# An encoder block on one core: the opening rebuilt in four column quarters, and the two first weight tiles of a norm three steps apart

## The chip, the core and the metric

The kernel runs on one core of a Trainium2 chip. Its engines are TensorE (PE: matmuls; PEld in the profile is its weight load), VectorE (DVE), ScalarE (ACT), GpSimd (POOL) and SyncE (SP, here only an issuer of transfers). Each works through its own list of instructions in order, and semaphores tie the lists together. SBUF is the working memory with 128 partitions, PSUM holds eight banks (pb0 to pb7) into which TensorE writes. The metric is the device time of one execution in microseconds (us), the median of several.

## What is computed

A residual block over 512 tokens of width 1024: a half-step SwiGLU FFN, a mixer (short convolution and latent attention), a second half-step FFN, a final norm. Each part is preceded by an RMS norm whose result is scaled and shifted by vectors that come from a conditioning vector c. What the change touches is the first three lines below.

```python
mod = (jax.nn.silu(c) @ ada_w[l] + ada_b[l]).reshape(b, N_MOD, D_MODEL)   # 1024 x 9216 weights
sh1, sc1, g1 = mod[:, 0], mod[:, 1], mod[:, 2]
h = modulate(rmsnorm(x, norm_ffn1_g[l]), sh1, sc1)          # h*(1+sc1)+sh1
x = x + 0.5 * g1[:, None, :] * swiglu(h, ffn1_w1[l], ffn1_w3[l], ffn1_w2[l])
h = modulate(rmsnorm(x, norm_mix_g[l]), sh2, sc2)
z = h @ w_in[l]
...
h = modulate(rmsnorm(x, norm_ffn2_g[l]), sh3, sc3)
x = x + 0.5 * g3[:, None, :] * swiglu(h, ffn2_w1[l], ffn2_w3[l], ffn2_w2[l])
return rmsnorm(x, final_norm_g)
```

## The kernel before

The order on every engine is written out by hand. x is kept transposed (features on partitions) as xres, eight tiles of 128x512. Every fp32 product is made from three matmuls of a faster number format (`three`, L711): a value is split into a high part and the rest, for weights (raw to wh on ACT in `split_hi`, then wl = raw - wh on DVE or GpSimd) and for activations (hh on ACT, hl on DVE). A weight tile ("unit") takes 8 steps of three matmuls with 512 columns. Two buffers of each kind alternate, so a unit's split waits until the unit two before it is done (unit_done).

The opening, up to the loop of FFN1:

- SP (L264 on) issues constants, positions, x in one transfer of 2 MB, ten small vectors and a constant, then ada_start in eight transfers of 1 MB (scale's 1024x1024 weights, then shift's), then the first two weight tiles raw0 and raw1.
- TensorE turns the vectors (L803) and x (L811, 32 transposes), copies going to xres on ACT (L465). It multiplies a part of the modulation weights itself: `ada_columns` (L813 to L822) takes k-tiles 0 and 1 of scale, and 0 to 2 of shift, with a 128x128 block of weights as the stationary operand and one column of silu(c) as the moving one.
- DVE accumulates the other k-tiles in acc (128x1024, `ada`, L1183 and L1185), then transposes in 32x32 blocks and reduces (`fold`, L1192, L1195), and TensorE adds up the rest (`mod_columns`, L834). `mod_bias` makes mods of it.
- ACT squares each tile of xres (L412), GpSimd adds the eight squares up (L357), TensorE sums over partitions (`norm_sum`, L736), ACT takes the root (L417), DVE the inverse, and `norm_spread` (L754) spreads it over the partitions into pb7.
- `apply` (L1158 and L1151): u = x * a * spread, hh = u + shift on ACT (L429), hl on DVE. The shift vector is made between tile 2 and tile 3 of u.
- Then `first_pair` (L763): the two first units, whose steps alternate, b = 0 and b = 1 for each k, as each tile of hh and hl comes. It is used three times: FFN1, the mixer's projection, FFN2.
- `warm` (L758) issues matmuls of 384 columns whose result is not used.

The loops of FFN1, FFN2 and their second halves then run with TensorE as the engine that sets the pace; the other seven modulation vectors are made in FFN1's loop from ada_ring, whose transfers GpSimd issues once mods_ready is 2.

## Time and profile before

| | us |
|---|---|
| median of 3 runs | 1050.64 |
| lowest, highest | 1049.11, 1053.35 |
| profiled execution, its own time | 1052.29 |
| span in it, first to last instruction | 1050.6 |
| TensorE busy | 1007.4 |
| DVE busy | 545.6 |
| ACT busy | 400.2 |

All durations below come from the one profiled execution. Between its span and its own time lie 1.7 us. Its time is 1.65 us above the median. "Idle before, releaser" in a row of the timeline gives how long the engine stood still before the instruction and what let it go. A merged row (x48) has the first start and the time to the last end.

### The profile page before, as it was taken

To read this page: it belongs to the slowest core of one execution; us is meant where nothing else is said; L and a number is where in the kernel's file an instruction comes from. 1 tells how busy PE (TensorE), PEld (TensorE's weight loads), DVE (VectorE), ACT (ScalarE), POOL (GpSimd) and SP (SyncE) were. 2 spreads that over 40 slices of the span, in tenths; PEclk is the share of its full clock that TensorE was granted. 3 is DMA by queue.
4 is the path that set the end of the run, shared out by engine and by line. 5 is a ranking of instruction groups with operands and counts; after the bars stand their busy time and mean duration, and the time that the engine had idled before them with its cause. 6 is when DMAs were issued, how large, how long until landed. Compare 5 with 4: busy or idle time off the path is not lost.

```text
span 1050.6 us, 13295 instructions
## 1 busy us (share of the span) xinstructions
PE 1007.4 (96%) x4551; PEld 833.3 (79%) x4551; DVE 545.6 (52%) x715; ACT 400.2 (38%) x568; POOL 66.0 (6%) x79
## 2 busy tenths in 40 slices
PE   3689999999999999999999999999999999999997
PEld 3668888888888888788877787878888888888886
DVE  5768777787753333644367634743334343333332
ACT  3244434444332222432255543444434444332222
POOL 2411111011000000000000311000000000000000
PEclk9599999999999999999999799999999999999999
DMA  9548766686623333223221102223333333333332
GB/s 332 177 134 250 241 198 209 208 258 219 218 88 98 92 90 112 54 81 92 79 75 41 41 14 68 80 80 100 100 100 91 89 99 100 95 93 92 90 110 80
DMA packets 176622, 127.82 MB, mean 122 GB/s; under 512 B 5069, under 2 KB 165718, under 8 KB 176598
## 3 DMA queue, kind: packets, MB, share of 16 engines
q1 hardware_dynamic: 168534, 98.14, 31.1%
q0 software_dynamic: 8064, 29.36, 8.4%
q8 instruction: 14, 0.23, 0.1%
q14 instruction: 10, 0.08, 0.0%
HBM read 125.39 MB, written 2.10 MB: 121 GB/s over the span
## 4 chain that ended last, share of the span: by engine, by line
PE 91%; DVE 1%; ACT 1%; issue 0%; DVEq 0%; ACTq 0%
PE pb L717 86%; PE pb L761 1%; PE pb L754 1%; PE pb L973 1%; PE pb L736 1%; PE pb L953 0%; DVE probs L1480 0%; PE pb L925 0%; ACT wh L403 0%; PE pb L747 0%; PE pb L744 0%; DVE wl L1119 0%; PE pb L1100 0%; DVE o_nat L1572 0%; PE pb L933 0%
## 5 line engine op out<-in xcount | busy, mean ns | idle before, releaser
L717 PE MATMUL pb<-hh,wh 128*128 128x512 f32 x912 | 358.2, 393 | 8.7 <-DVE sbuf L1221 4.7
L717 PE MATMUL pb<-hh,wl 128*128 128x512 f32 x912 | 355.6, 390 | 0.0
L717 PE MATMUL pb<-hl,wh 128*128 128x512 f32 x912 | 355.6, 390 | 0.0
L1119 DVE TENSOR_TENSOR wl<-raw,wh 128x1024 fp32r<-128x1024 f32 x156 | 191.0, 1224 | 281.2 <-ACT wh L403 281.2
L403 ACT ACTIVATE wh<-raw 128x1024 fp32r<-128x1024 f32 x163 | 172.4, 1058 | 410.5 <-PE pb L717 410.5
L717 PEld LDWEIGHTS pb<-hh,wh 128*128 128x128 f32 x912 | 171.5, 188 | 47.5 <-DVE sbuf L1221 5.5
L717 PEld LDWEIGHTS pb<-hh,wl 128*128 128x128 f32 x912 | 171.6, 188 | 36.1
L717 PEld LDWEIGHTS pb<-hl,wh 128*128 128x128 f32 x912 | 171.7, 188 | 35.0
L717 PE MATMUL pb<-gh,wh 128*128 128x512 f32 x352 | 137.0, 389 | 0.0
L717 PE MATMUL pb<-gh,wl 128*128 128x512 f32 x352 | 136.9, 389 | 0.0
L717 PE MATMUL pb<-gl,wh 128*128 128x512 f32 x352 | 136.9, 389 | 0.0
L717 PEld LDWEIGHTS pb<-gh,wh 128*128 128x128 f32 x352 | 66.1, 188 | 13.9
L717 PEld LDWEIGHTS pb<-gh,wl 128*128 128x128 f32 x352 | 66.1, 188 | 13.8
L717 PEld LDWEIGHTS pb<-gl,wh 128*128 128x128 f32 x352 | 66.1, 188 | 13.5
L1185 DVE SCALAR_TENSOR_TENSOR acc<-ada_ring,silu_c,acc 128x1024 f32<-128x1024 f32 x49 | 62.8, 1282 | 1.0
L1227 DVE TENSOR_TENSOR gbuf<-sbuf,pb 128x512 f32<-128x512 f32 x44 | 30.1, 685 | 58.4 <-PE pb L717 58.3
L440 ACT ACT_TABLE_LOAD x44 | 56.5, 1283 | 0.8
L412 ACT ACTIVATE sq<-xres 128x512 f32<-128x512 f32 (+1 forms) x32 | 20.2, 631 | 90.5 <-DVE xres L1237 85.5
L368 POOL DMA_DIRECT2D ada_ring<-in_ada_w_dram x56 | 29.7, 531 | 211.6 <-DVE acc L1183 113.0
L1237 DVE SCALAR_TENSOR_TENSOR xres<-pb,half_gates,xres 128x512 f32 (+1 forms) x16 | 12.0, 751 | 46.6 <-PE pb L717 46.6
L447 ACT ACTIVATE gh<-gbuf 128x512 f32 x44 | 27.9, 633 | 13.3 <-DVE gbuf L1227 13.3
L1230 DVE TENSOR_TENSOR gl<-gbuf,gh 128x512 f32 (+1 forms) x44 | 30.1, 683 | 0.0
(193 smaller groups left out, 745.6 us busy)
## 6 DMA issues: line engine op xcount, KB each, us to landing
raw<-in_ffn_w_dram SPq DMA_DIRECT2D x104, 512.0 KB, 3.7
ada_ring<-in_ada_w_dram POOLq DMA_DIRECT2D x56, 512.0 KB, 5.3
raw<-in_ffn_w_dram SPq DMA_DIRECT2D x32, 448.0 KB, 3.4
raw<-in_w_in_dram SPq DMA_DIRECT2D x17, 512.0 KB, 3.7
ada_start<-in_ada_w_dram SPq DMA_DIRECT2D x8, 1024.0 KB, 16.4
raw<-in_w_out_dram SPq DMA_DIRECT2D x8, 512.0 KB, 3.4
x_nat<-in_x_dram SPq DMA_DIRECT2D x1, 2048.0 KB, 10.5
out_dram<-o_nat SPq DMA_DIRECT2D x8, 256.0 KB, 2.9
```

Of the source, the lines that this page charges most:

```text
L368: pool.dma_start(ada_ring[:, k % 4, :], adav[:, k, bass.ds(j * D_MODEL + 2 * D_MODEL, D_MODEL)]) \
L403: act.activation(wh[par][:, :], raw[par][:, :], ACT.Copy).then_inc(hi_ready, 1)
L412: act.activation(sq[:, slot, :], src, ACT.Square).then_inc(sq_ready, 1)
L440: act.activation(vcol[:, V_COLS + 9:V_COLS + 10], kst[:, K_COLS:K_COLS + 1], ACT.Sigmoid)
L447: act.activation(gh[:, bass.ds(i, 1), :], gbuf[:, :].unsqueeze(1), ACT.Copy).then_inc(gh_ready, 1)
L717: last = pe.matmul(o, a, b, start=start and j == 0 and t == 0, stop=stop and j == len(pairs) - 1 and t == 2)
L736: last = pe.matmul(norm_bank[:, t:t + 1], src[:, t * P:(t + 1) * P], one_col, start=True, stop=True)
L1119: dve.tensor_tensor(wl[par][:, :], raw[par][:, :], wh[par][:, :].bitcast(F32), ALU.subtract).then_inc(lo_ready, 1)
L1185: dve.scalar_tensor_tensor(out=acc[:, :], in0=src, scalar=silu_c[:, k:k + 1], in1=acc[:, :], op0=ALU.mult, op1=ALU.add).then_inc(ada_step, 1)
L1227: dve.tensor_tensor(gbuf[:, :], sbuf[:, :], pb[1][:, :], ALU.mult).then_inc(g_ready, 1)
L1230: dve.tensor_tensor(gl[:, bass.ds(i, 1), :], gbuf[:, :].unsqueeze(1), gh[:, bass.ds(i, 1), :].bitcast(F32), ALU.subtract).then_inc(gl_read ...
L1237: dve.scalar_tensor_tensor(out=xd, in0=pb[bank][:, :].unsqueeze(1), scalar=gate, in1=xd, op0=ALU.mult, op1=ALU.add).then_inc(x_upd, 1)
```

## The change

The opening is made anew. x comes in four transfers by token block, each with a semaphore. The ten vectors and the second constant are issued by ACT instead of SP. The modulation weights for scale and shift come in four groups g = 0 to 3 (scale low, shift low, scale high, shift high; low and high are halves of 512 columns), in four transfers each, with raw0 between g0 and g1 and raw1 between g1 and g2. Of each group TensorE takes k-tiles 0, 2, 4, 6 (`start_cols`, 16 matmuls), DVE 1, 3, 5, 7 at half width (`start_chunk`), and TensorE then sums DVE's partial vector with a column of ones (`start_sum`, 4 matmuls) into the same PSUM bank. The transpose, the reduction and their small matmul are gone from the opening. The squares are taken by ACT on x as it came, one token block each, with an accumulated sum per token (`token_squares`), so that GpSimd's adds and `norm_sum` are gone. u goes into the memory of hl (u_first). After the low halves of scale and shift TensorE does steps 0 to 3 of the first weight tile, then groups 2 and 3, then steps 0 to 3 of the second tile, steps 4 to 7 of the first, steps 4 to 7 of the second. `first_pair`, now used in the mixer and FFN2 only, runs the second tile three steps behind the first.

```diff
         def _(sp):
...
-            sp.dma_start(x_nat[:, :, :], x[0].rearrange("(t p) d -> p t d", p=P)).then_inc(x_landed, 16)
+            for t in range(TT):
+                sp.dma_start(x_nat[:, t, :], x[0][t * P:(t + 1) * P, :]).then_inc(x_landed[t], 16)
+
+            def start_load(g):
+
+                v, half = g % 2, g // 2
+                col = (D_MODEL if v == 0 else 0) + half * HALF_COLS
+                for i in range(4):
+                    sp.dma_start(ada_start[:, DT * v + 2 * i:DT * v + 2 * i + 2, half * HALF_COLS:(half + 1) * HALF_COLS],
+                                 adav[:, 2 * i:2 * i + 2, col:col + HALF_COLS]).then_inc(start_landed[g][i], 16)
...
         def _(pool):
-            pool.wait_ge(sacc_clear, 1)
-            for k in range(DT):
-                pool.wait_ge(sq_ready, k + 1)
-                pool.wait_ge(sq_added, k)
-                pool.tensor_tensor(sacc[:, :], sacc[:, :], sq[:, k % 2, :], ALU.add).then_inc(sq_added, 1)
...
+            def token_squares(t):
+
+                act.wait_ge(x_landed[t], 16)
+                if t > 0:
+                    act.wait_ge(tokens_squared, t)
+                act.activation(turned[:, :], x_nat[:, t, :], ACT.Square, accum_out=ssq[:, t:t + 1]).then_inc(tokens_squared, 1)
+
+            token_squares(0)
+            token_squares(1)
             act.wait_ge(vec_ready, 3)
             act.activation(sig_c[:, :], vcol[:, V_C:V_C + DT], ACT.Sigmoid).then_inc(sigc_ready, 1)
-            act.wait_ge(cs_step, 10)
-            act.activation(cs[:, :], ang[:, :], ACT.Sin).then_inc(cs_ready, 1)
+            sqrt_table(6)
+            token_squares(2)
+            token_squares(3)
+            act.wait_ge(tokens_squared, TT)
+            act.activation(rms[:, :], ssq[:, :], ACT.Sqrt, scale=1.0 / D_MODEL, bias=kst[:, K_COLS:K_COLS + 1]).then_inc(rms_ready, 1)
             for k in range(DT):
                 act.wait_ge(x_turned, k + 1)
-                act.activation(xres[:, k, :], pb[k % 4][:, :], ACT.Copy).then_inc(x_copied, 1)
-                act.wait_ge(x_copied, k + 1)
-                square(N_FFN1, k, k % 2, xres[:, k, :])
...
+                act.activation(xres[:, k, :], pb[X_BANK[k]][:, :], ACT.Copy).then_inc(x_copied, 1)
...
             def first_pair(base, hbase):
 
-                for k in range(DT):
-                    for b in range(2):
-                        if k == 0:
+                for k in range(DT + LAG):
+                    for b, kb in ((0, k), (1, k - LAG)):
+                        if not 0 <= kb < DT:
+                            continue
+                        if kb == 0:
                             unit(base + b)
...
-                last = three(pb[b][:, :], [(cols(wh[b], k), cols(wl[b], k), hh[:, k, :], hl[:, k, :])],
-                                     k == 0, k == DT - 1)
+                        last = three(pb[b][:, :], [(cols(wh[b], kb), cols(wl[b], kb), hh[:, kb, :], hl[:, kb, :])],
+                                     kb == 0, kb == DT - 1)
...
+            def start_cols(g, k):
+
+                v, half = g % 2, g // 2
+                pe.wait_ge(start_landed[g][k // 2], 16)
+                for col in range(HALF):
+                    at_ = half * HALF_COLS + col * P
+                    pe.matmul(pb[1 + g][:, col:col + 1], ada_start[:, DT * v + k, at_:at_ + P], silu_c[:, k:k + 1],
+                              start=k == ADA_ON_PE[0] and col == 0, stop=False, skip_group_check=True)
+
+            def start_sum(g):
+
+                v = g % 2
+                pe.wait_ge(start_step, len(ADA_ON_DVE) * (g + 1))
+                for col in range(HALF):
+                    at_ = v * HALF_COLS + col * P
+                    last = pe.matmul(pb[1 + g][:, col:col + 1], acc[:, at_:at_ + P], one_col,
+                                     start=False, stop=True, skip_group_check=True)
                 last.then_inc(ada_direct, 1)
 
             pe.wait_ge(siluc_ready, 1)
-            ada_columns(0)
-            pe.wait_ge(sq_added, DT)
-            norm_sum(N_FFN1, sacc, 0)
+            for g in range(2):
+                pe.wait_ge(x_copied, g + 2)
+                for k in ADA_ON_PE:
+                    start_cols(g, k)
+                    if g == 0 and k == ADA_ON_PE[1]:
+                        pe.wait_ge(vec_ready, 3)
+                        norm_spread(N_FFN1)
+                start_sum(g)
...
+            warm(WARM_START, 6)
+            unit(U_A1)
+            pe.wait_ge(x_copied, DT)
+            first_steps(0, range(HALF))
+            for g in range(2, 4):
+                for k in ADA_ON_PE:
+                    start_cols(g, k)
+                start_sum(g)
+            unit(U_A1 + 1)
+            pe.wait_ge(ada_direct, 1)
+            first_steps(1, range(HALF))
+            first_steps(0, range(HALF, DT)).then_inc(unit_done, 1)
+            first_steps(1, range(HALF, DT)).then_inc(unit_done, 1)
...
             def first_u(k):
...
             start_chunk(0, 1)
             inverse(N_FFN1)
+            for k in (3, 5, 7):
+                start_chunk(0, k)
+            start_mod(0)
+            for k in ADA_ON_DVE:
+                start_chunk(1, k)
+                first_u(k // 2)
+            start_mod(1)
+            for k in range(HALF):
+                first_lo(k)
+            for k in ADA_ON_DVE:
+                start_chunk(2, k)
+            start_chunk(3, 1)
+            start_chunk(3, 3)
+            start_mod(2)
+            start_chunk(3, 5)
+            start_chunk(3, 7)
+            first_u(4)
+            first_u(5)
+            start_mod(3)
```

The next two pieces are TensorE's list in the opening, from the first modulation matmul on (x4 and the like count matmuls of the program; the name behind "waits" is the semaphore). Before:

```order
L821 MATMUL pb<-silu_c,ada_start 128x1 [waits start_landed0,siluc_ready]
L821 MATMUL pb<-silu_c,ada_start 128x1 x15
L736 MATMUL pb<-kst,sacc 128x1 [waits sq_added]
L736 MATMUL pb<-kst,sacc 128x1 x3
L834 MATMUL pb<-folded,kst 128x32 [waits mods_ready,ada_folded,vec_ready]
L754 MATMUL pb<-kst,rrms 128x128 [waits rrms_ready,exact_ready]
L754 MATMUL pb<-kst,rrms 128x128 x3
L821 MATMUL pb<-silu_c,ada_start 128x1 [waits start_landed5,start_landed4]
L821 MATMUL pb<-silu_c,ada_start 128x1 x23
L761 MATMUL pb<-exact 128x384 x7
```

All of it stood before the first product. Of the change, group 0 alone:

```order
L857 MATMUL pb<-silu_c,ada_start 128x1 [waits start_landed0_0,x_copied,siluc_ready]
L857 MATMUL pb<-silu_c,ada_start 128x1 x3
L857 MATMUL pb<-silu_c,ada_start 128x1 [waits start_landed0_1]
L857 MATMUL pb<-silu_c,ada_start 128x1 x3
L780 MATMUL pb<-kst,rrms 128x128 [waits rrms_ready,vec_ready]
L780 MATMUL pb<-kst,rrms 128x128 x3
L857 MATMUL pb<-silu_c,ada_start 128x1 [waits start_landed0_2]
L857 MATMUL pb<-silu_c,ada_start 128x1 x3
L857 MATMUL pb<-silu_c,ada_start 128x1 [waits start_landed0_3]
L857 MATMUL pb<-silu_c,ada_start 128x1 x3
L866 MATMUL pb<-kst,acc 128x1 [waits start_step]
L866 MATMUL pb<-kst,acc 128x1 x3
```

Four such groups (the spread only in the first) stand in place of the 40 matmuls and the two folded sums; two of them, and the 12 products between, follow the warm-up.

On DVE, from the third quarter on, the change has this:

```order
L1363 SCALAR_TENSOR_TENSOR acc<-ada_start,silu_c,acc 128x512 [waits start_step,start_landed3_1]
L1371 TENSOR_TENSOR mods<-pb,vcol 128x4 [waits ada_direct]
L1379 SCALAR_TENSOR_TENSOR a_cols<-mods,vcol 128x4 [waits start_mods]
L1363 SCALAR_TENSOR_TENSOR acc<-ada_start,silu_c,acc 128x512 [waits start_step,start_landed3_2,cols_ready]
L1363 SCALAR_TENSOR_TENSOR acc<-ada_start,silu_c,acc 128x512 [waits start_step,start_landed3_3]
L1388 SCALAR_TENSOR_TENSOR u_first<-xres,a_cols,pb 128x512 [waits x_copied] x2
```

The wait for TensorE's third sum (ada_direct) stands ahead of DVE's last two steps of the fourth group.

The third place is first_pair in FFN2 on TensorE, behind its warm-up. Before, with bank pb0 for the first weight tile and pb1 for the second:

```order
L717 MATMUL pb0<-hl_51,wh0_54 128x512
L717 MATMUL pb0<-hh_50,wl0_56 128x512
L717 MATMUL pb1<-hh_50,wh1_55 128x512
L717 MATMUL pb1<-hl_51,wh1_55 128x512
L717 MATMUL pb1<-hh_50,wl1_57 128x512
L717 MATMUL pb0<-hh_50,wh0_54 128x512
```

Each step of pb0 is followed by the same step of pb1. In the change, from the third step of pb0 on:

```order
L743 MATMUL pb0<-hl_51,wh0_54 128x512
L743 MATMUL pb0<-hh_50,wl0_56 128x512
L743 MATMUL pb0<-hh_50,wh0_54 128x512
L743 MATMUL pb0<-hl_51,wh0_54 128x512
L743 MATMUL pb0<-hh_50,wl0_56 128x512
L743 MATMUL pb1<-hh_50,wh1_55 128x512
```

The first step of pb1 comes behind the fourth of pb0, and at the end four steps of pb1 stand alone.

## Rows read from the trace of the kernel before

**Rows 1.** The page: span, engine line of TensorE, granted clock in 40 slices.

```profile
span 1050.6 us, 13295 instructions
PE 1007.4 (96%) x4551; PEld 833.3 (79%) x4551; DVE 545.6 (52%) x715; ACT 400.2 (38%) x568; POOL 66.0 (6%) x79
PEclk9599999999999999999999799999999999999999
```

**Rows 2.** FFN1's loop: start:end, length, busy time by engine, clock, DMA share, GB/s.

```profile
105.00:200.00 95.00, 94.77 (x420) 78.37 (x419) 71.77 (x80) 39.19 (x50) 12.67 (x24) 1.00 0.72 227
```

**Rows 3.** Timeline of TensorE: start, us, operation, idle before and releaser.

```profile
14.06 0.42 PE L803 MATMUL pb<-kst,vec 112*128 112x112 f32 x1 [14.06 <-DMA vec<-in_conv_w_dram]
...
14.64 5.00 PE L811 MATMUL pb<-kst,x_nat 128*128 128x128 f32 x24
...
21.77 3.63 PE L821 MATMUL pb<-silu_c,ada_start 128*128 128x1 f32 x32
34.02 1.87 PE L736 MATMUL pb<-kst,sacc 128*128 128x1 f32 x8 [8.61 <-POOL sacc L357]
...
36.65 2.08 PE L754 MATMUL pb<-kst,rrms 128*128 128x128 f32 x8 [0.29 <-ACT exact L471]
38.52 10.24 PE L821 MATMUL pb<-silu_c,ada_start 128*128 128x1 f32 x48
48.62 2.59 PE L761 MATMUL pb<-exact 128*128 128x384 f32 x7
...
68.00 0.50 PE L717 MATMUL pb<-hh,wh 128*128 128x512 f32 x1 [2.33 <-DVE sbuf L1221]
```

**Rows 4.** Timeline of DVE: the angle's last step, accumulation in opening and loop.

```profile
10.94 0.43 DVE L1279 TENSOR_SCALAR ang<-posf 128x512 f32<-128x512 f32 x1
...
20.52 10.90 DVE L1185 SCALAR_TENSOR_TENSOR acc<-ada_start,silu_c,acc 128x1024 f32<-128x1024 f32 x5
...
77.39 2.61 DVE L1185 SCALAR_TENSOR_TENSOR acc<-ada_ring,silu_c,acc 128x1024 f32<-128x1024 f32 x2
```

**Rows 5.** Stretches of 1 us, TensorE alone: busy, clock, DMA share, GB/s.

```profile
25.00:26.00 1.00, 0.40 (x4) 0.80 1.07 426
...
52.00:53.00 1.00, 1.00 (x5) 0.55 0.00 0
```

**Rows 6.** Transfers: x issued, KB, us to landing; the second raw tile issued; its landing.

```profile
x_nat<-in_x_dram SPq DMA_DIRECT2D x1, 2048.0 KB, 10.5
...
21.07 9.72 SPq L317 DMA_DIRECT2D raw<-in_ffn_w_dram  x1
DMA to landing us min/median/max: 16.4/16.4/16.4
```

**Rows 7.** ACT: copy of a tile, table load, accumulator's reading, split of a weight tile.

```profile
17.20 0.58 ACT L465 ACTIVATE xres<-pb 128x512 f32<-128x512 f32 x1
31.09 1.28 ACT L422 ACT_TABLE_LOAD   x1
L579 ACT ACTIVATION_READ_ACCUMULATOR probs<-pb,nmax_s x16: 191/194/209, 559.4 to 611.6; 128x1 f32 x16
65.03 1.06 ACT L403 ACTIVATE wh<-raw 128x1024 fp32r<-128x1024 f32 x1 [2.16 <-PE pb L717]
```

**Rows 8.** FFN2's first pair and behind it: DVE's hl, ACT's split, TensorE's next unit.

```profile
677.75 0.75 DVE L1151 SCALAR_TENSOR_TENSOR hl<-ubuf,mods,hh 128x512 fp32r<-128x512 f32 x1
...
679.07 0.75 DVE L1151 SCALAR_TENSOR_TENSOR hl<-ubuf,mods,hh 128x512 fp32r<-128x512 f32 x1
...
686.50 1.06 ACT L403 ACTIVATE wh<-raw 128x1024 fp32r<-128x1024 f32 x1 [1.11 <-PE pb L717]
...
689.47 0.50 PE L717 MATMUL pb<-hh,wh 128*128 128x512 f32 x1 [2.32 <-DVE sbuf L1221]
```

**Rows 9.** TensorE behind the mixer's first pair.

```profile
440.59 0.50 PE L717 MATMUL pb<-hh,wh 128*128 128x512 f32 x1 [1.79 <-DVE wl L1119]
...
442.13 0.63 PE L717 MATMUL pb<-hh,wh 128*128 128x512 f32 x1
...
444.69 0.63 PE L717 MATMUL pb<-hh,wh 128*128 128x512 f32 x1
```

192 lines of the change are left out of this document (116 added, 76 removed).

## The prediction

> **What bounds the kernel now.** The page comes first: its span is 1050.6 us, TensorE is busy for 96% of it, and the clock line is full almost everywhere but in the second of forty slices [rows 1]. A stretch of the first FFN (105 to 200 us) holds 420 large matmuls in 94.77 busy us, 0.226 us each, without a gap [rows 2]. Such a loop can't be shortened by what DVE or ACT do beside it; it can only start earlier. The one part where TensorE isn't the bound is the opening, so I read its timeline next: transposes of x from 14.64, one-column matmuls of the modulation from 21.77, their second part of 10.24 us from 38.52, warm-up from 48.62, then the first pair of weight tiles, and the loop from 68.00 [rows 3]. What counts is when the loop can start. Everything behind 68.00 is moved with it, except at the two other places where first_pair is used.
>
> In the opening TensorE waits for DVE (two vectors accumulated, five instructions in 10.90 us, 2.18 us each, while GpSimd adds squares; 1.3 us each when it doesn't [rows 4]), and then DVE waits for nothing but its own list. That is what the change takes apart. But the clock must be read with it: it fell at about 25.8 us and came back at about 52.9 us [rows 5]. The 48 records of one-column work lie wholly between: 10.24/48 = 0.213 us each, against 3.63/32 = 0.113 us at 21.77, at the full clock [rows 3]. TensorE was busy without a pause from 38.5 to 48.8 and the clock stayed at 1.2 GHz; it rose only 4.3 us after the 384-column warm-up began.
>
> The Trainium skill (TensorE: Matmul & The Clock Gate, Why this matters for your kernels) advises to keep TensorE continuously busy to have its faster clock. By that rule the new chain of one-column matmuls would run fast; the rows just named say that for this shape it doesn't. What the rule would give is the first rival below.
>
> **The change, part by part.** One program matmul of this kind is two records, so 0.43 us at the low clock and 0.23 at the high one. Before, 16+24 of them and two short sums of a folded vector were TensorE's share, with the transpose and reduction on DVE. After, there are four groups (scale low, shift low, scale high, shift high) of 16 weight matmuls and 4 sums over DVE's partial vector: 80 matmuls. The price of a group at the low clock is 32 x 0.213 = 6.83, and a sum of four is 1.87 (the squares' sum has just that form [rows 3]): 8.70 us. At the high clock it is 3.63 + 0.94 = 4.57 us (the sum halved, an estimate).
>
> Start of the chain. x as one transfer lands at 1.80 + 10.5 = 12.3 us [rows 6]; in four parts the last lands then too, the first by about 8.4 (a quarter each 1.3 us). The vector loads go to ACT's queue and no longer stand behind x. Before they landed at 14.06 [rows 3]; I take 8 to 10, and anything up to 10.8 is hidden, since DVE's angle work ends at 11.4 [rows 4] and its copy of the vectors stands behind it. ACT: squares of tokens 0 and 1 to 10.9 (1.06 each for a 1024-column pass, 0.19 for the accumulator's reading), sigmoid's table to 12.2, sigmoid to 12.4, the root's table 1.28 and dummy 0.2, squares of tokens 2 and 3 at 1.25, root 0.26, two copies of 0.58 [rows 7]: 12.4+1.5+2.5+0.3+1.2 = 17.9. There the first group may write its bank.
>
> First half on TensorE, at the low clock: 6.83 + 2.08 (spread of 1/rms, same row as before) + 1.87 = 10.8, then 8.7: 17.9 to 37.4. DVE's four half-width steps per group (0.65 each) and the transfers are hidden behind TensorE: between 12.3 and 37.5 (where the second raw tile landed, 21.07 + 16.4 [rows 6]) the same bytes pass in the new order, shift low being complete about half way, at 25, 10 us before it is used up, and the last quarter at 37.5, 15 us before. So the 2 KB rows of the new transfers, the removed squares on GpSimd, the removed transpose and reduction and the sine moved behind the copies cost and bring nothing on the path: TensorE is its own bound. Would it not be, the last quarter's landing would be next. On SP's queue the second and third raw tile lie further back or behind all quarters, and are wanted only at 43 and later. On GpSimd's, the two splits no longer follow the adds, and the ring's first four loads wait for the shift's high half (about 57, against the first pair's start before, so a few us later); DVE uses them only in the loop's first tile, some 10 us behind its start.
>
> Then a warm-up of 2.6 us to 40.0 (shift, hi and lo of tile 0 are ready by then: two passes of the size of DVE's hl, 0.75 [rows 8], and a short one after 37.4), and 12 matmuls of the first weights. With the clock up 4.3 us after 37.4, four run at 0.427 us (the spacing at the low clock: six from 442.13 to 444.69 [rows 9]) and eight at 0.226: until 43.5. The clock held for 3.9 us after the transposes before ended (from 21.8, where one-column work takes over, to 25.8), so until about 47.4: group three costs 4.6, to 48.1, and group four 8.7 at the low clock, to 56.9. Bounds: never falling, 43.5 + 9.1 = 52.6; low for both, 60.9.
>
> Then 36 matmuls. The clock rises 4.3 us later again: 10 at 0.427, 26 at 0.226, to 67.0; unhindered they need 8.1, if the rise takes half as long again (6.5 us, my margin) 11.4. The first weights are complete 12 matmuls (2.7 us) earlier, at 64.3. From there to the loop's first matmul takes 2.97 us (ACT's split at 65.03, loop at 68.00 [rows 3, 7]), so **the loop starts at 67.3, against 68.0: 0.7 us gained.** DVE's high half (two u, shift, hi, lo) is ready at 61.5 to 63, before TensorE wants it.
>
> Lag in first_pair. Before, DVE gives a tile each 1.32 us (677.75 to 679.07) and TensorE needs 6 x 0.226 = 1.36 for both products [rows 8], so they ran in step. With the second product three tiles behind, TensorE idles about 0.6 us three times, and three more second-weight tiles (2.0 us) lie behind the last first-weight one. That one ends about 0.3 us sooner (ACT's split at 686.50 before), and the 2.97 us to the next unit (689.47) is now covered by 2.7 us of matmuls where it was a 2.3 us stall [rows 8]. The two effects nearly cancel: 0.3 us gained in FFN2, 0.2 us in the mixer's pair, where the stall was 1.79 us. Behind that stall the clock was low for seven matmuls, 7 x 0.2 = 1.4 us [rows 9]; without the stall it may not be. Bounds for a place: the clock falling in the new idle spots instead, 1.4 lost; dip and stall gone, 1.7 gained.
>
> **Sum.** Profiled execution: 1052.29 - 0.7 - 0.5 = 1051.1, and 1049.7 if the mixer's dip goes. This execution lies 1.65 us above the median, which may be that dip, so I don't count it against the median: 1050.64 - 1.2 = **1049.4 us**.
>
> **Rivals.**
> 1. The clock stays high for one-column work. Then the transfers bound it: 37.5 + 0.7 + 0.9 + 8.1 and about 2 us for a rise, loop at 49 to 50, time about 1032. Against it stand the 10.24 us. Chance 0.07.
> 2. The dense transposes (about 8.4 to 14.8, then four at 17) raise the clock, and it holds 3.9 us past the last: until about 21.5. Then 17.9 to 21.5 passes nearly twice the work, 3.5 us saved: 1045.9, and less if DVE and ACT are ahead of my sum. For it: 21.77 to 25.4 ran high behind transposes. Against: the gap from 14.8 to 17 wasn't there. Chance 0.20.
> 3. Slower: groups three and four both at the low clock, because the dense stretch before them (warm-up and 12 matmuls, 6 us) is too short to hold it, and a late rise behind. Place: 43 to 61 us. The fourth sum ends at 60.9, the pair at 72.3, and the loop starts at 72.6, 4.6 late; less the lag's 0.5: 1054.7. It decides against the kernel once the fourth sum ends after 58.1 (loop at 68.5). Chance 0.17.
> 4. The vectors on ACT's queue land as late as they did, 14.06: everything from the sigmoid on is 2.7 us later, 1052.1. Chance 0.08.
> 5. The lag's idle spots lower the clock in both pairs, 2 x 1.4: 1052.2. Chance 0.06.
> The forecast itself keeps 0.42.
>
> **How the numbers follow.** About 0.5% (5.3 us) is what a measurement of this kernel can tell from no change: below 1045.4 or above 1055.9. Rival 1, half of rival 2 and a little of the forecast lie below: 0.20. A quarter of rival 3, and 4 or 5 with it, lie above: 0.06. The rest, 0.74, is no change. The range takes rivals 2 to 5 whole and leaves out the first: 1043.5 to 1055.
>
> **What would show it.** In the profile after: one-column rows with a mean start to start of 0.21 us in the first two groups, and TensorE without idle time from 18 to 37; the first 384-column matmul near 37; the fourth sum's end near 57; the loop's first matmul near 67; first_pair in FFN2 with three idle spots of 0.6 us and no 2.3 us stall behind it. I am wrong if the clock is high between 18 and 37, if TensorE waits there for a landing or for DVE, or if the vectors land after 10.8.

## The result and the profile after

| | before | after |
|---|---|---|
| median of the runs | 1050.76 us (20 runs, 1048.70 to 1055.64) | 1046.95 us (20 runs, 1040.72 to 1049.02) |
| ratio to before, 95% interval | | 0.9949 [0.9937, 0.9961] |
| profiled execution, own time (span) | 1052.29 (1050.6) us | 1044.10 (1042.4) us |
| loop's first matmul in it | 68.00 us | 63.70 us |

The medians differ by 3.8 us (0.36%). The ratio, which is formed from runs of both kernels made side by side, is 0.51% below one, with an interval from 0.39% to 0.63%. So the result is a gain that is clear of noise. It lies inside the prediction's range and 2.5 us below its value; by the ratio it is just past the bound of 0.5% between no change and faster, by the median (1046.95 against 1045.4) short of it.

The page of the kernel after: the span, the engine line of TensorE, and the granted clock in 40 slices of 26 us.

```profile
span 1042.4 us, 13409 instructions
PE 1014.9 (97%) x4612; PEld 841.1 (81%) x4612; DVE 533.0 (51%) x717; ACT 400.8 (38%) x569; POOL 51.8 (5%) x71
PEclk8689999999999999999999899999999999999999
```

TensorE is busy for 7.5 us longer than in [rows 1] and the span is 8.2 us shorter, so its idle time fell by 15.7 us. The low clock now shows in the first three slices, where before it was the second alone. By stretches of 0.1 us it lasts from 20.3 to 37.4 us and from 44.2 to 57.8, 30.7 us in all, against 27.3 before (25.6 to 52.9). So the opening's gain isn't less time at the low clock.

The timeline of TensorE in the kernel after, the opening (start, us, engine line operation, tiles, shape, count, and in brackets the idle time before and who ended it). It answers to [rows 3]:

```profile
17.70 1.92 PE L857 MATMUL pb<-silu_c,ada_start 128*128 128x1 f32 x16
...
23.88 1.85 PE L866 MATMUL pb<-kst,acc 128*128 128x1 f32 x8
25.59 6.97 PE L857 MATMUL pb<-silu_c,ada_start 128*128 128x1 f32 x32
32.41 1.85 PE L866 MATMUL pb<-kst,acc 128*128 128x1 f32 x8
34.12 2.59 PE L787 MATMUL pb<-exact 128*128 128x384 f32 x7
36.51 0.63 PE L743 MATMUL pb<-hh,wh 128*128 128x512 f32 x1
...
39.66 3.63 PE L857 MATMUL pb<-silu_c,ada_start 128*128 128x1 f32 x32
...
44.04 6.86 PE L857 MATMUL pb<-silu_c,ada_start 128*128 128x1 f32 x32
50.76 1.85 PE L866 MATMUL pb<-kst,acc 128*128 128x1 f32 x8
52.47 0.77 PE L743 MATMUL pb<-hh,wh 128*128 128x512 f32 x1
...
57.73 0.44 PE L743 MATMUL pb<-hh,wh 128*128 128x512 f32 x1
...
63.70 0.50 PE L743 MATMUL pb<-hh,wh 128*128 128x512 f32 x1 [0.29 <-DVE sbuf L1281]
```

No row of the timeline from 17.70 up to the gap of 0.29 us at 63.70 has a bracket: TensorE is the bound of its opening, as the prediction said. The four groups of 32 records and a sum of 8 are easy to find. The 32 records took 6.97 us in the second group and 6.86 in the fourth, but 3.63 in the third: the same work at two clocks. So the reader wants the clock next, in stretches of the kernel after, TensorE alone (stretch, length, busy time and records, granted clock, DMA share, GB/s). Its first stretch answers to [rows 5]:

```profile
24.00:36.00 12.00, 12.00 (x55) 0.50 1.07 373
36.00:40.00 4.00, 4.00 (x19) 0.83 0.69 206
40.00:44.00 4.00, 4.00 (x38) 1.00 0.46 131
...
48.00:56.00 8.00, 8.00 (x30) 0.50 0.10 27
...
105.00:200.00 95.00, 94.87 (x421) 1.00 0.72 227
418.00:450.00 32.00, 30.96 (x153) 1.00 0.21 58
```

TensorE was busy in every microsecond from 20 to 36 and from 44 to 56 and, but for the first 0.3 us of each, stood at the lower of its two levels there, 1.2 GHz. The FFN's loop (105 to 200) is what it was [rows 2].

**Where the 8.2 us of this pair of executions went.** I took the same instruction in both timelines at several places and subtracted:

| place | before | after | shift | what came on |
|---|---|---|---|---|
| loop's first matmul | 68.00 | 63.70 | 4.30 | opening |
| mixer's first pair starts | 427.66 | 423.14 | 4.52 | 0.2 |
| heads, before the first dip | 573.34 | 567.00 | 6.34 | 1.8: the mixer's pair |
| heads, ten us on | 585.15 | 577.28 | 7.87 | 1.5: a dip of the clock that the run after didn't have |
| FFN2's first pair starts | 676.00 | 667.93 | 8.07 | 0.2 |
| unit behind it | 689.47 | 681.26 | 8.21 | 0.14: FFN2's pair |

The fourth row is no effect that the code explains: here is the stretch in the kernel before, where the clock was low in part, and the one that answers to it in the kernel after.

```profile
570.00:580.00 10.00, 9.21 (x45) 0.83 0.00 0
```

```profile
560.00:570.00 10.00, 9.22 (x52) 1.00 0.07 25
```

So the profiled pair shows more than the medians do: before's execution lay 1.5 us above its median, after's 2.9 below. Every experiment below is read in the same way, by its own time less its loop start.

### The profile page after: what moved, and what is told of

Its sections match the earlier page's. It is cut to its first block, busy times and chain, and to the rows that moved or that the text cites. A ratio compares the mean times of both kernels' runs of the same rounds, so it can differ in the third digit from the quotient of the medians.

```text
span 1042.4 us, 13409 instructions
## 1 busy us (share of the span) xinstructions
PE 1014.9 (97%) x4612; PEld 841.1 (81%) x4612; DVE 533.0 (51%) x717; ACT 400.8 (38%) x569; POOL 51.8 (5%) x71
## 4 chain that ended last, share of the span: by engine, by line
PE 89%; DVE 2%; issue 1%; ACT 1%; DVEq 0%; ACTq 0%
PE pb L743 86%; PE pb L780 1%; PE pb L762 1%; DVE hl L1211 1%; DVE ubuf L1218 1%; PE pb L787 0%; PE pb L1033 0%; PE pb L985 0%; PE pb L1013 0%; DVE ubuf L1559 0%; PE pb L773 0%; PE pb L770 0%; PE pb L1160 0%; ACT wh L396 0%; DVE o_nat L1688 0%
## 5 line engine op out<-in xcount | busy, mean ns | idle before, releaser
L743 PEld LDWEIGHTS pb<-gl,wh 128*128 128x128 f32 x352 | 66.1, 188 | 13.8
L405 ACT ACTIVATE sq<-xres 128x512 f32 (+1 forms) x24 | 15.2, 632 | 85.7 <-DVE xres L1297 85.6
L440 ACT ACTIVATE gh<-gbuf 128x512 f32 x44 | 27.9, 634 | 10.8 <-DVE gbuf L1287 10.7
```

The lines of the kernel that those rows point to most:

```text
L405: act.activation(sq[:, slot, :], src, ACT.Square).then_inc(sq_ready, 1)
L440: act.activation(gh[:, bass.ds(i, 1), :], gbuf[:, :].unsqueeze(1), ACT.Copy).then_inc(gh_ready, 1)
L743: last = pe.matmul(o, a, b, start=start and j == 0 and t == 0, stop=stop and j == len(pairs) - 1 and t == 2)
```

## The experiments

Each experiment changes the kernel after, except the second one, which changes the kernel before. Ratios are to the kernel before, on the same chip.

| kernel | median us | ratio [95%] | loop starts | own time | own less loop start |
|---|---|---|---|---|---|
| before | 1050.76 | 1 | 68.00 | 1052.29 | 984.29 |
| after | 1046.95 | 0.9949 [0.9937, 0.9961] | 63.70 | 1044.10 | 980.40 |
| e1_opening_alone | 1048.51 | 0.9973 [0.9955, 0.9991] | 65.03 | 1048.35 | 983.32 |
| e2_lag_alone | 1050.38 | 0.9988 [0.9976, 1.0001] | 67.98 | 1050.26 | 982.28 |
| e3_two_on_pe | 1042.90 | 0.9917 [0.9896, 0.9938] | 60.68 | 1042.90 | 982.22 |
| e4_one_on_pe | 1044.89 | 0.9935 [0.9914, 0.9956] | 63.37 | 1045.50 | 982.13 |
| e5_x_whole | 1050.92 | 1.001 [0.9996, 1.0024] | 69.84 | 1050.28 | 980.44 |
| e6_16_more | 1054.60 | 1.0046 [1.0029, 1.0063] | 70.20 | 1052.37 | 982.17 |
| e7_balanced | 1040.38 | 0.9911 [0.9894, 0.9928] | 59.43 | 1039.86 | 980.43 |
| e8_no_warm | 1048.91 | 0.998 [0.9965, 0.9996] | 66.58 | 1046.88 | 980.30 |
| e9_four_in_second | 1038.84 | 0.9895 [0.9872, 0.9918] | 56.72 | 1038.92 | 982.20 |
| e10_three_in_third | 1039.12 | 0.9889 [0.9873, 0.9906] | 59.19 | 1039.71 | 980.52 |

The last column is the main reading of the study. In the nine kernels that have both the new opening and the lag, the work behind the loop's start took 980.3 to 980.5 us or 982.1 to 982.2, over loop starts that range from 56.72 to 70.20. What the opening does to the loop's start comes out at the end one for one, and nothing gives it back. The step of 1.8 us between the two values is near the price of one dip of the clock (about 1.6 us, below), and the traces show which dip: in the four kernels with 982.1 to 982.2 the clock fell in the stretch of the fourth row above (at 561.8 us in e9, 566.1 in e3, 568.5 in e4, 575.3 in e6), as it did before at 575.1, and in none of the five others.

**The opening alone.** The lag taken out of the kernel after:

```diff
-LAG = 3
+LAG = 0
```

> The changed kernel with the new opening, but first_pair in the mixer and FFN2 alternates step by step as before (lag 0). By the sum of the prediction the lag is worth 0.5 us (0.3 in FFN2, 0.2 in the mixer), up to 1.9 us if the mixer's stall of 1.8 us and the low clock behind it come back: 0.5 to 2 us slower than the changed kernel, about 1048 us, and both stalls (1.8 and 2.3 us) are in the profile again. Rival, that the lag costs (three idle spots in which the clock falls): 1 to 3 us faster than the changed kernel, 1044 to 1046.

The stalls behind the pairs are back as in [rows 8, 9]. Two rows of TensorE's timeline in this kernel, behind the mixer's pair and behind FFN2's, and a third, 1.7 us on from the first, with the long matmul that marks the low clock:

```profile
437.36 0.50 PE L743 MATMUL pb<-hh,wh 128*128 128x512 f32 x1 [1.79 <-DVE wl L1179]
...
439.06 0.63 PE L743 MATMUL pb<-hh,wl 128*128 128x512 f32 x1
...
685.55 0.50 PE L743 MATMUL pb<-hh,wh 128*128 128x512 f32 x1 [2.33 <-DVE sbuf L1281]
```

The opening alone is worth 0.27% of the time, 2.8 us, and the median of 1048.51 is as expected. In this execution the clock fell earlier in the first group, at about 18.2 us instead of 20.3, and the group took longer: its first 16 records 2.78 us, where they took 1.92 in after. Its first group spans 17.40 to 26.87, 9.5 us, where after's spans 17.70 to 25.59, 7.9. That is an effect of when the clock falls, not of the lag, which acts 350 us later. So after's 63.70 is a good execution of the new opening, and 65.03 another one.

**The lag alone**, written into `first_pair` of the kernel before, for the mixer and FFN2 (FFN1 keeps the old order):

```diff
-            def first_pair(base, hbase):
+            def first_pair(base, hbase, lag=3):
...
-                for k in range(DT):
-                    for b in range(2):
-                        if k == 0:
+                for k in range(DT + lag):
+                    for b, kb in ((0, k), (1, k - lag)):
+                        if not 0 <= kb < DT:
+                            continue
+                        if kb == 0:
...
-            first_pair(U_A1, AP_BASE[N_FFN1])
+            first_pair(U_A1, AP_BASE[N_FFN1], 0)
```

> The kernel before with the lag of three steps in the mixer's and FFN2's first_pair only; the opening and its pair are as before. By the prediction 0.5 us faster than before, up to 1.9 if the mixer's clock dip goes: 1049 to 1050.3 us. If the lag carries most of the gain of the change: 3 us or more, below 1048. If its idle spots lower the clock: up to 1053.5.

0.12% with an interval that just holds no change, and a median at the edge of what I expected. The trace says what the lag does. From the first matmul of FFN2's pair to the unit behind it: 674.17 to 687.48, 13.31 us, against 676.00 to 689.47, 13.47 us before and 667.93 to 681.26, 13.33 us after. In the mixer the same stretch is 12.89 us here (429.14 to 442.03) and 12.93 before (427.66 to 440.59). So the reordering itself saves 0.16 and 0.04 us, 0.2 in all. What it does more is behind the pair: no dip of the clock there. But this execution had one at another stall of the same kind, in front of FFN1's loop, which neither change touches here. TensorE's timeline of this kernel:

```profile
67.98 0.79 PE L717 MATMUL pb<-hh,wh 128*128 128x512 f32 x1 [2.32 <-DVE sbuf L1223]
...
71.14 0.46 PE L717 MATMUL pb<-hl,wh 128*128 128x512 f32 x1
```

Between the two rows the matmuls stand 0.43 us apart and behind them 0.23. The eight from 67.98 to 71.43 took 3.45 us, where the kernel before needs 1.95 (68.00 to 69.95): 1.5 us lost. The kernel before has the same stall of 2.33 us at 68.00 [rows 3] and didn't have the dip in its profiled execution; it had one behind the mixer's stall of 1.79 us [rows 9], and so had the first experiment. A stall of about 2 us is thus followed by a dip in some executions and not in others. In the new opening that first stall is 0.29 us, with the lag the mixer's is gone too, and that is one way in which the whole change is worth more than its parts' 0.27% and 0.12% (0.39% together, against 0.51%). The intervals overlap, though, so I don't call the surplus shown.

**Less on TensorE: two k-tiles of eight instead of four**, DVE takes six.

```diff
-ADA_ON_PE, ADA_ON_DVE = (0, 2, 4, 6), (1, 3, 5, 7)
+ADA_ON_PE, ADA_ON_DVE = (0, 4), (1, 2, 3, 5, 6, 7)
```

> TensorE takes k-tiles 0 and 4 of each group instead of 0, 2, 4, 6; DVE takes the other six. If TensorE's one-column matmuls at the low clock are the bound of the opening: a group is 16 records x 0.213 = 3.4 us shorter, the chain 11 to 13 us shorter, until DVE (about 0.66 us a step, two more steps a group) or the last landing at 37.5 us is the bound, fourth sum near 46.5 instead of 52.5, loop at 57 to 58, time 1041. If transfers or DVE were the bound of the opening already: no gain or 1 to 5 us slower than the changed kernel.

**And one k-tile**, DVE takes seven.

```diff
-ADA_ON_PE, ADA_ON_DVE = (0, 2, 4, 6), (1, 3, 5, 7)
+ADA_ON_PE, ADA_ON_DVE = (0,), (1, 2, 3, 4, 5, 6, 7)
```

> TensorE takes only k-tile 0 of each group, DVE seven. TensorE's group is 1.7 + 1.9 us. By the theory DVE is now the bound: 28 steps, 8 u and 8 hl one after the other, so no further gain over two tiles, loop at 56 to 59, time 1040 to 1043; DVE without idle time from 23 to 46 us and TensorE waiting for it. If TensorE's count alone set the end, another 6 us would go: 1035.

With two, the kernel is 4 us faster than after by the medians, and the loop starts 3.0 us earlier. With one it is 2 us slower again than with two. The sums of the two kernels tell why. TensorE's timeline with two k-tiles:

```profile
30.89 1.87 PE L866 MATMUL pb<-kst,acc 128*128 128x1 f32 x8 [4.76 <-DVE acc L1363]
...
48.33 1.87 PE L866 MATMUL pb<-kst,acc 128*128 128x1 f32 x8 [0.38 <-DVE acc L1363]
```

and with one:

```profile
31.57 1.87 PE L866 MATMUL pb<-kst,acc 128*128 128x1 f32 x8 [6.49 <-DVE acc L1363]
...
51.27 1.87 PE L866 MATMUL pb<-kst,acc 128*128 128x1 f32 x8 [2.95 <-DVE acc L1363]
```

In the kernel after none of the sums waits. With two k-tiles three of them wait for DVE, 4.76, 2.68 and 0.38 us, 7.8 in all. But 64 records are gone, 12.0 us by the rates of the two clocks (48 at 0.213, 16 at 0.113), so 4.2 are left over; 3.0 came against after's execution and 4.35 against the first experiment's. With one, all four wait, 1.80, 6.49, 3.63 and 2.95 us, 14.9 in all: DVE is the bound in every group. The best split lies between, and it isn't the same in each group. Both kernels fell short of what I had expected (loops at 57 to 58 and at 56 to 59, fourth sum near 46.5 with two k-tiles): the loops started at 60.68 and 63.37, the fourth sum of the first at 48.33. Part of it is DVE's pace in the third group, where five accumulations took 6.11 us beside GpSimd's split of a weight tile, and five took 4.19 in the first group (more on this in the last section).

**x in one transfer**, as before the change.

```diff
-        x_landed = [sem(f"x_landed{t}") for t in range(TT)]
+        x_landed = [sem("x_landed0")] * TT
...
-            for t in range(TT):
-                sp.dma_start(x_nat[:, t, :], x[0][t * P:(t + 1) * P, :]).then_inc(x_landed[t], 16)
+            sp.dma_start(x_nat[:, :, :], x[0].rearrange("(t p) d -> p t d", p=P)).then_inc(x_landed[0], 16)
```

> The changed kernel with x in one transfer again (one semaphore, landing near 11.5 to 12.3 us). The chain of the opening starts with ACT's token squares, so it starts later: the four squares, two table loads, the sigmoid and the root behind the landing give the second copy of x near 20.5 to 21.5 instead of 17.7. If TensorE is the bound from there on, the loop starts 3 to 4 us later (67 to 68) and the time is 1050 to 1051 us, the gain of the opening gone. If it isn't, under 1 us is lost.

The whole gain is gone: ratio 1.001. ACT's timeline of this kernel: the first pass of squares, the root, and the copies of x, of which the second lets TensorE begin its first group.

```profile
13.10 1.06 ACT L469 ACTIVATE turned<-x_nat 128x1024 f32<-128x1024 f32 x1 [5.51 <-DMA x_nat<-in_x_dram]
...
21.05 3.50 ACT L482 ACTIVATE xres<-pb 128x512 f32<-128x512 f32 x7
```

In the kernel after the squares begin at 8.35 and the copies at 16.54 (its rows stand in the next section). Here they begin 4.75 and 4.51 us later, TensorE's first group starts at 22.21 instead of 17.70, and the loop at 69.84 instead of 63.70. The chain of squares, tables, root and first copy is as long in both, 8.0 us here (13.10 to 21.05) and 8.2 in after (8.35 to 16.54); with four transfers it begins on the first part. The prediction had this cut in its sum, in the start at 17.9, but gave it no price of its own. By this run it carries the opening's whole gain: without it the new opening is no faster than the old one. The clock's share must be kept apart, since group 0 took 9.44 us here (22.21 to 31.65) and 7.89 in after. The first experiment's execution, whose group 0 took 9.47, is the better partner: against it the first group starts 4.81 us later and the loop 4.81 us later (69.84 against 65.03). I had expected the loop at 67 to 68; the first squares started 0.8 us after the latest landing that I had taken, and group 0 was the slow kind.

**More on TensorE**: 16 additional one-column matmuls in the second group, whose results go to a bank that nothing reads. It is the same work as one more group of k-tiles. That bank first holds the seventh tile of the transposed x, so the second group also waits until ACT has copied seven tiles instead of three.

```diff
-                pe.wait_ge(x_copied, g + 2)
+                pe.wait_ge(x_copied, g + 2 if g == 0 else 7)
...
+                    if g == 1:
+                        for col in range(HALF):
+                            pe.matmul(pb[6][:, col:col + 1], ada_start[:, DT + k, col * P:(col + 1) * P],
+                                      silu_c[:, k:k + 1], start=True, stop=True)
```

> The changed kernel with 16 more one-column matmuls in group 1, into a bank nobody reads; nothing else is added. If TensorE is the bound and they run at the low clock: 16 x 2 x 0.213 = 6.8 us later, loop at 70.5, 1053.8 us. If DVE or the landings set the pace: 0 to 2 us. If they ran at the high clock: 3.6 us.

TensorE's timeline of this kernel, from the second group to the warm-up behind it:

```profile
26.23 1.85 PE L857 MATMUL pb<-silu_c,ada_start 128*128 128x1 f32 x8
27.94 1.84 PE L880 MATMUL pb<-silu_c,ada_start 128*128 128x1 f32 x8
...
41.59 2.59 PE L787 MATMUL pb<-exact 128*128 128x384 f32 x7
```

The row at 26.23 has no bracket, so the changed wait held nothing up. The group spans 26.23 to 41.59, 15.36 us against 8.53 in after: 6.83 us more for 32 records, 0.213 us each, the prediction's price to the digit. The loop starts 6.5 us later and the median is 7.7 us longer. Whatever is put on TensorE there is paid in full.

**Without the warm-up.**

```diff
-            warm(WARM_START, 6)
```

> The changed kernel without the 7 warm-up matmuls of 384 columns before the first product (2.6 us of TensorE). If the warm-up earns the clock for group three: the 12 products run at the low clock until 41, and group three at the low clock in part or whole: 1.3 to 5 us slower, 1048 to 1052. If the 12 products would raise it soon enough by themselves: within 1.3 us of the changed kernel.

TensorE's timeline of this kernel:

```profile
36.91 0.77 PE L743 MATMUL pb<-hh,wh 128*128 128x512 f32 x1 [1.96 <-DVE hl L1393]
...
42.17 3.99 PE L857 MATMUL pb<-silu_c,ada_start 128*128 128x1 f32 x32
```

Without the seven 384-column matmuls TensorE waits 1.96 us for DVE, so some 0.6 of the 2.59 us could have been saved. Instead all twelve products of the first weights ran at the low clock, 36.91 to 42.17, 5.3 us where after needs 3.2 (36.51 to 39.66), and the median rose by 2 us. Of the 2.9 us by which the loop starts later in this execution 0.7 came before, in group 0 (its end is at 26.29, against 25.59), and have nothing to do with the warm-up. The warm-up fills 2 us of wait, costs about 0.6 us beyond it, and brings the clock's rise forward, which is worth more.

**A balanced version.** From what the third and the fourth experiment showed, group by group: TensorE takes 2, 3, 4 and 2 k-tiles of the four groups. The split of the second weight tile goes ahead of the first normalised tiles on ACT, so that GpSimd's part of it is over before DVE's third and fourth groups. These are two changes in one run, and no run takes them apart. Its lines besides renumbering:

```diff
-ADA_ON_PE, ADA_ON_DVE = (0, 2, 4, 6), (1, 3, 5, 7)
+ADA_ON_PE = ((0, 4), (0, 2, 4), (0, 2, 4, 6), (0, 4))
+ADA_ON_DVE = tuple(tuple(k for k in range(8) if k not in p) for p in ADA_ON_PE)
...
+            split_hi(1, 1, 16)
             act.wait_ge(start_mods, 3)
             for k in range(HALF):
                 first_hi(k)
-            split_hi(1, 1, 16)
```

> TensorE takes 2, 3, 4 and 2 k-tiles of groups 0 to 3 (DVE 6, 5, 4, 6), and ACT splits the second raw tile before the first hi parts, so that GpSimd's split of it (2.5 us at 38, beside which DVE's steps took 1.2 to 1.5 us instead of 0.66) falls into a time in which DVE waits. By the theory: second sum ends near 32, group three near 42.5, fourth sum near 47 (50.2 in the kernel with two tiles everywhere), loop at 57 to 58, 1039 to 1041 us. If GpSimd's split isn't what slows DVE there, or the clock falls earlier: 1043, as with two tiles everywhere.

It beats both the kernel before and the kernel after: 1040.38 us, ratio 0.9911 [0.9894, 0.9928], 6.6 us (0.6%) below the kernel after. Against two k-tiles everywhere (1042.90, 0.9917 [0.9896, 0.9938]) the intervals cover each other. TensorE's timeline:

```profile
31.37 1.87 PE L868 MATMUL pb<-kst,acc 128*128 128x1 f32 x8 [3.64 <-DVE acc L1365]
...
48.01 0.77 PE L745 MATMUL pb<-hh,wh 128*128 128x512 f32 x1
```

Against after, the first group gives 2.9 us (17.45 to 22.47, against 17.70 to 25.59), the fourth 3.6 (43.20 to 48.01, against 44.04 to 52.47). The second loses 2.1, with its 3.64 us wait for DVE. That wait is why the loop starts later (59.43) than I had expected: in the second group DVE's list also holds the four steps of u, and I had given DVE one k-tile too many there. That is an argument so far, and the next run tries it. DVE's last accumulation of that group shows what made it so dear:

```profile
29.14 2.18 DVE L1365 SCALAR_TENSOR_TENSOR acc<-ada_start,silu_c,acc 128x512 f32<-128x512 f32 x1
```

It took 2.18 us where the one before it (27.81) took 0.75. GpSimd's split, which this kernel had moved forward, ran from 28.37 to 30.76, beside it.

**Four k-tiles in the second group**, so 2, 4, 4, 2 on TensorE.

```diff
-ADA_ON_PE = ((0, 4), (0, 2, 4), (0, 2, 4, 6), (0, 4))
+ADA_ON_PE = ((0, 4), (0, 2, 4, 6), (0, 2, 4, 6), (0, 4))
```

> TensorE takes 2, 4, 4, 2 k-tiles of the four groups (the balanced kernel 2, 3, 4, 2). In the balanced kernel the second sum waited 3.64 us for DVE at 31.37. If DVE's list sets the end of that group (my theory), one accumulation fewer brings the sum 0.66 us forward and TensorE's 1.7 us of additional matmuls lie within the wait, which shrinks to about 1.3 us: loop at about 58.8 instead of 59.43, median about 1039.7. Rival: TensorE's one-column work is paid in full as in the kernel with 16 more: loop 1.7 us later, at 61.1, median 1042.

The second sum doesn't wait any more. Its row in TensorE's timeline of this kernel:

```profile
29.76 1.84 PE L868 MATMUL pb<-kst,acc 128*128 128x1 f32 x8
```

It starts at 29.76 instead of 31.37, 1.6 us sooner though TensorE has 8 records more in the group. So DVE's list set the end there, and the rival (TensorE's work paid in full) is out for this group. The gain is larger than the 0.66 us that I had taken, because the accumulation that went is the one that took 2.18 us beside GpSimd's split; DVE's last one of the group is now over at 28.65, 1.1 us before the sum. The loop starts 2.7 us earlier (56.72), but 1.0 of it is the clock, which rose 3.5 us behind the product at 46.34 here and 5.8 us behind the one at 48.01 in the balanced kernel. The median is 1.5 us lower: 1038.84, ratio 0.9895 [0.9872, 0.9918], the lowest median of the study, 8.1 us below the kernel after. From the balanced kernel's ratio it can't be told apart.

**Three in the third group**, so 2, 4, 3, 2.

```diff
-ADA_ON_PE = ((0, 4), (0, 2, 4), (0, 2, 4, 6), (0, 4))
+ADA_ON_PE = ((0, 4), (0, 2, 4, 6), (0, 2, 4), (0, 4))
```

> 2, 4, 3, 2 k-tiles. In addition to the last kernel one k-tile less of the third group, which runs at the high clock: 8 records of 0.113 us, 0.9 us. DVE has 5 accumulations in that group, done at about 40.6, before the sum at about 40.7, so it should just not wait: loop at about 57.9 and median about 1038.8. Rival: the fourth group's accumulations, which DVE does behind them, become late, and its sum waits about 0.7 us for DVE: loop at 58.5 to 58.8, no gain.

No gain over the last one: 1039.12 against 1038.84, with intervals that cover each other. The gain that I had put first didn't come, and the rival's reason for that, a fourth sum that waits for DVE, wasn't the cause: no sum waits for DVE in this kernel. But the clock fell within the third group: its 24 records took 3.10 us (37.83 on) and its sum 1.85, where the last kernel has 3.63 for 32 and 1.03. The group needed 4.67 us with three k-tiles and 4.38 with four. The loop started 2.5 us later than in the last kernel's execution (59.19), half of it by a later rise of the clock behind the fourth group; that the medians agree all the same shows how much a single execution's loop start holds of the clock. Whether the clock fell early by chance in this execution, or because of the shorter run of work, one trace doesn't tell.

## Why the prediction was right, step by step

The value was 1049.4 and the measured median 1046.95; range, side and the likeliest case held. The mechanism was right, the size was not: a gain of 1.2 us was forecast and 3.8 came, by the terms below. The steps compared with the trace of the kernel after:

| step | predicted | after | opening alone (e1) |
|---|---|---|---|
| first group starts | 17.9 | 17.70 | 17.40 |
| group 0 with the spread | 10.8 | 7.89 | 9.47 |
| group 1 | 8.7 | 8.53 | 8.53 |
| warm-up and 12 matmuls | 6.1 | 5.54 | 5.58 |
| group 2 | 4.6 | 4.38 | 4.38 |
| group 3 | 8.7 | 8.43 | 8.37 |
| from there to the loop | 10.4 | 11.23 | 11.3 |
| loop starts | 67.3 | 63.70 | 65.03 |

**The chain and its bound: right.** TensorE has no idle time from 17.7 on, groups 1 to 3 are priced to 0.3 us, and the experiments with 16 matmuls more and with fewer show it as cause and not only as picture. That the one-column matmuls run at the low clock for most of the way (rival 1 against it, chance 0.07) was the step on which most hung, and the rows are plain: 25.59 to 32.41 is 32 records of 0.213 us. The Trainium skill (TensorE: Matmul & The Clock Gate, Why this matters for your kernels) advises to keep TensorE continuously busy to have its faster clock. In this case's trace TensorE was continuously busy from 25.6 to 34.1 with matmuls of this shape and its clock stayed at 0.50, so for them the measurement disagrees.

**The term that was mis-sized: group 0.** I had it wholly at the low clock, 10.8 us. It took 7.89, because the clock was high at its start and fell only at about 20.3: the 16 records of 17.70 took 1.92 us at the high clock. That is the mechanism of rival 2 (chance 0.20), which priced it at 3.5 us; 2.9 came. In the first experiment's execution it fell at about 18.2 and 1.3 us came. Against it I had set a gap between 14.8 and 17. That gap didn't come: in after the transposes of x run until 16.3 and the pause is 0.89 us, since the later parts of x land later. In the ten executions of the new opening the fall lay 0.8 to 2.6 us behind the start of the first group (after 20.3, e3 20.0, e7 19.7, e10 19.5, e9 19.1, e6 and e8 19.0, e4 18.9, e1 18.2, and e5 23.1 with its later chain). So a part of rival 2, 1 to 3 us, belonged in the forecast. Here are ACT's rows of the kernel after at the start of the chain. They show that my sum of 17.9 was made of the right parts:

```profile
8.35 1.06 ACT L470 ACTIVATE turned<-x_nat 128x1024 f32<-128x1024 f32 x1 [0.53 <-DMA x_nat<-in_x_dram]
...
16.34 0.30 ACT L480 ACTIVATE rms<-ssq,kst 128x4 f32<-128x4 f32 x1
16.54 3.98 ACT L483 ACTIVATE xres<-pb 128x512 f32<-128x512 f32 x8
```

The hold itself was taken from a single execution. I had read 3.9 us behind the transposes (by stretches of 0.1 us the clock fell at 25.6, not 25.8). In the second experiment's execution, whose opening is the old one, it fell at 23.5, 1.7 us behind them, and the 32 records took 5.27 us instead of 3.63.

**The clock's rise.** From the warm-up I took 4.3 us, as in the trace before. In after it came sooner: the matmul of 37.36 is the first short one, 3.2 us behind 34.12. That is the 0.56 us in the fourth row. In the last stretch it came later, 5.3 us behind 52.47: 12 products stood 0.43 us apart instead of the ten that I had. That is most of the 0.8 us lost there. The two nearly cancel. (The prediction's 11.4 us for a late rise comes out as 11.2 by its own rates; nothing hangs on it.) Rival 3 (a late rise behind groups three and four) didn't come: group 2 began at the high clock in all executions but the one without the warm-up. It didn't always hold: in e10 the clock fell at 40.0, within the group, in e4 at 42.8, while its sum waited for DVE, and in e3 at 43.9, within its sum.

**The vectors** landed at 10.94, later than the 8 to 10 I took, and 0.14 us past the bound of 10.8 below which I called it harmless. DVE's angle work ended later too, at 11.7, so DVE's copy didn't wait for them: right by its mechanism, wrong by its number. The prediction had named a landing after 10.8 as a sign of being wrong, and a high clock between 18 and 37 as another. Both came in part, and the second is the mis-sized term above; the third, a wait of TensorE for a landing or for DVE, didn't. Rival 4 (14.06) didn't come.

**The lag** I had at 0.5 us. The same stretches give 0.14 to 0.16 us in FFN2 and 0.04 in the mixer, 0.2 together. The three idle spots are there. TensorE's timeline of after in FFN2's pair, which answers to [rows 8]:

```profile
669.16 0.50 PE L743 MATMUL pb<-hh,wh 128*128 128x512 f32 x1 [0.30 <-DVE hl L1211]
...
669.73 0.40 PE L743 MATMUL pb<-hh,wl 128*128 128x512 f32 x1
670.48 0.51 PE L743 MATMUL pb<-hh,wh 128*128 128x512 f32 x1 [0.35 <-DVE hl L1211]
...
681.26 0.50 PE L743 MATMUL pb<-hh,wh 128*128 128x512 f32 x1 [0.29 <-DVE sbuf L1281]
```

The bracket says 0.30 to 0.35 us, but the three products start at 669.16, 669.50 and 669.73 and the next at 670.48, 0.75 later where 0.23 would do: 0.5 to 0.6 us are lost at each, as the sum had it. The 2.3 us stall is 0.29. They cancel almost wholly. The dip behind the mixer's stall, for which the prediction kept a second sum, is gone, as the stretch 418 to 450 with clock 1.00 shows: it was 1.6 us in the trace before (nine matmuls in 3.65 us, 441.85 to 445.50, where 2.05 would do), and this "maybe" looks like the larger part of what the lag brings (the first experiment is 0.24% slower than after, the lag's own 0.2 us are 0.02%). The intervals of these two kernels still touch, at 0.9955 and 0.9961, so the size of that part isn't shown. Rival 5 (idle spots lower the clock) didn't come.

**The sum.** By the profiled executions the terms put right are 1052.29 - 4.3 - 0.2 - 1.6 = 1046.2, and 1047.5 with the first experiment's opening (3.0 us). After's own time was 1044.10. Of the 2.1 us left 1.5 are the dip in the heads' stage, and the rest is spread over the kernel in pieces of 0.2. Against the median I had counted 1.2 us; 3.8 came, of which the opening is 2.8 by the first experiment's ratio. The range was said to take rival 3 whole, yet a quarter of it was counted above 1055.9, past the range's end at 1055; the result lies far from there.

**Why the fall comes at 18.2 in one execution and at 20.3 in another.** The transposes show it, in after (two rows) and in the first experiment (one):

```profile
11.54 4.74 PE L830 MATMUL pb<-kst,x_nat 128*128 128x128 f32 x21
17.17 0.66 PE L830 MATMUL pb<-kst,x_nat 128*128 128x128 f32 x4 [0.89 <-ACT xres L483]
```

```profile
11.38 4.17 PE L830 MATMUL pb<-kst,x_nat 128*128 128x128 f32 x21
```

The 21 transposes of after stand 0.21 us apart and the last four 0.11 to 0.17: the first ran at the low clock, and it rose only between the two groups. (The clock column of the stretches reads 1.00 from the start of the span, ahead of the first change that the trace holds; the rows say otherwise.) In the first experiment the rise came within the 21, which took 4.17 us. An early rise went with an early fall: the 21 took 4.17 us where it fell at 18.2 (e1), 4.48 to 4.69 where it fell at 18.9 to 19.1 (e6, e4, e8, e9), and 4.74, none of them fast, where it fell at 19.5 to 20.3 (e10, e7, e3, after). So group 0 gets what is left of a short high stretch that begins in the transposes.

**What stays open.** What sets the moment of that rise isn't shown. Nor is it shown what decides whether a 2 us stall is followed by a dip. And after's 20 runs spread over 8 us, which I put down to these two without having traced them all.

## What to carry to other kernels

Where a serial opening hands work from engine to engine, find the one that never waits, price its work at the clock that rows of the same shape show, and move the split until both sides wait a little: here four k-tiles of eight gained 0.5%, and a split by group of 2, 4, 4, 2 (with one split of a weight tile moved forward) gained 1.05%. A gain at the start of a loop that is bound by one engine reaches the end one for one, and a change of order within a bound stretch is worth next to nothing, unless it takes away a stall behind which the clock may fall. Cut the first transfer so that work can begin on its first part: that alone carried the opening's gain here.

## What the runs showed of the hardware that I had not expected

**The clock on one-column work.** In after the clock held through the first 2.6 us of group 0 (17.7 to 20.3, the spread's matmuls among them) and through 4.5 us of one-column work later (39.7 to 44.2), each time after dense matmuls. In between it stayed low through 13.8 us (20.3 to 34.1) of back-to-back one-column matmuls. The same 32 records cost 3.63 or 6.97 us. Work of that shape should be priced at the second figure unless dense work stands right in front.

**DVE beside GpSimd.** DVE's three accumulations of 512 columns took 4.38 us in the kernel after, where GpSimd splits a weight tile at the same time, and 2.46 us in the balanced kernel, where the split came 9 us earlier. DVE's and GpSimd's timelines, of the kernel after:

```profile
38.57 4.38 DVE L1363 SCALAR_TENSOR_TENSOR acc<-ada_start,silu_c,acc 128x512 f32<-128x512 f32 x3
38.15 2.54 POOL L353 TENSOR_TENSOR wl<-raw,wh 128x1024 fp32r<-128x1024 f32 x1 [13.85 <-ACT wh L396]
```

and of the balanced one:

```profile
37.54 2.46 DVE L1365 SCALAR_TENSOR_TENSOR acc<-ada_start,silu_c,acc 128x512 f32<-128x512 f32 x3
28.37 2.39 POOL L355 TENSOR_TENSOR wl<-raw,wh 128x1024 fp32r<-128x1024 f32 x1 [4.31 <-ACT wh L398]
```

DVE lost 1.92 us of the 2.1 us in which the two overlapped (38.57 to 40.69). The Trainium skill (SBUF — State Buffer, Who interferes with whom) says that a DVE instruction with two inputs in SBUF contends with a GpSimd instruction that reads SBUF. By that rule, the trace agrees: both are of that kind here. So does the accumulation of 2.18 us in the balanced kernel, while a step of u beside the same split (28.48, 0.74 us), one of whose two inputs is in PSUM, isn't slower than the others. In the kernel after it costs nothing, since TensorE is the bound. With six or seven k-tiles on DVE, or with the split moved beside DVE's last accumulation of the second group, it lies on the path.
